# Packed attention scores, a later compressed branch, and moved angle, norm and down-product work in a hybrid attention and expert kernel

## The reference

```
h = RMSNorm(x);  proj = h @ w_in
A: 8 query heads, 2 kv heads, window 128, learned sinks, rotary      -> o_a
B: 8 query heads, 2 kv heads, rotary, three gated branches           -> o_b
     compressed: 31 blocks of 32 keys -> MLP (gelu, hidden 256) -> one key, one value each
     selected:   top 16 blocks of 64 keys (with 512 tokens that is every block)
     window:     512 keys
x = x + concat(o_a, o_b) @ w_out
x = x + PEER(RMSNorm(x)):  q = h @ w_query;  per head top 16 of 128 x 128 product keys,
     gelu(h . expert_down[e]) * gate, summed over expert_up[e]
y = RMSNorm(x) * norm_f
```

## Time and profile before

| | |
|---|---|
| time, median of 3 runs | 1576.52 us (1574.54 to 1577.93) |
| time of the profiled execution | 1576.16 us |
| its span | 1574.3 us |
| TensorE busy | 1530.9 us, 97% |
| VectorE busy | 1228.3 us, 78% |
| ScalarE busy | 613.6 us, 39% |
| GpSimd busy | 493.5 us, 31% |
| DMA | 374.27 MB, mean 238 GB/s |

### The profile page before, as it was taken

How to read it: one execution, slowest core, us unless ns; L and a number is a source line. 1 busy time by engine, 2 the same in 40 slices (tenths; PEclk the granted TensorE clock), 3 DMA queues, 4 the chain that set the end, 5 groups by cost and what they waited for, 6 DMA issues and landing times.

```text
span 1574.3 us, 22581 instructions
## 1 busy us (share of the span) xinstructions
PE 1530.9 (97%) x8493; PEld 1352.7 (86%) x8493; DVE 1228.3 (78%) x2289; ACT 613.6 (39%) x1033; POOL 493.5 (31%) x323
## 2 busy tenths in 40 slices
PE   7998999999999989999999999999999999999997
PEld 5876887888889989999888887999999999999996
DVE  6637766347999999993766765889888889888986
ACT  6215554352221335663333333333333333333334
POOL 0000000215674830002111111555554555555520
PEclk9999999999999999999999999999999999999999
DMA  4510000423321547899998998999999999999971
GB/s 176 214 54 1 2 1 1 177 100 118 128 71 59 169 134 278 319 339 330 310 311 294 304 307 292 348 366 358 372 362 365 350 365 361 375 360 362 354 256 67
DMA packets 147164, 374.27 MB, mean 238 GB/s; under 512 B 11728, under 2 KB 76368, under 8 KB 144112
## 3 DMA queue, kind: packets, MB, share of 16 engines
q1 hardware_dynamic: 99488, 197.66, 36.3%
q0 software_dynamic: 37200, 138.56, 24.0%
q10 hardware_dynamic: 10368, 36.60, 6.2%
HBM read 334.11 MB, written 38.67 MB: 237 GB/s over the span
## 4 chain that ended last, share of the span: by engine, by line
PE 70%; DVE 25%; DMA 3%; issue 1%; ACT 1%; SPq 0%; ACTq 0%; DVEq 0%
PE bank L1651 30%; PE bank L1344 30%; PE bank L1429 3%; PE bank L1510 2%; DMA a_e<-act_dram 2%; DVE oh L1245 2%; DVE oh L1248 2%; DVE gp L1250 2%; DVE gp L1253 2%; DVE cand L1183 1%; DVE d_lo L1234 1%; PE bank L1494 1%; DVE key L1138 1%; DVE work L1158 1%; DVE ti L1157 1%
## 5 line engine op out<-in xcount | busy, mean ns | idle before, releaser
L1344 PE MATMUL bank<-h_hi,d_hi 128*128 128x384 f32 x1024 | 348.9, 341 | 2.8 <-DVE d_lo L1234 1.7
L1344 PE MATMUL bank<-h_lo,d_hi 128*128 128x384 f32 x1024 | 346.5, 338 | 0.0
L1344 PE MATMUL bank<-h_hi,d_lo 128*128 128x384 f32 x1024 | 346.2, 338 | 0.0
L1651 PE MATMUL bank<-u_hi,w_hi_e 128*128 128x512 f32 x768 | 301.3, 392 | 5.1 <-DVE u_lo L1229 5.1
L1651 PE MATMUL bank<-u_lo,w_hi_e 128*128 128x512 f32 x768 | 300.9, 392 | 0.0
L1651 PE MATMUL bank<-u_hi,w_lo_e 128*128 128x512 f32 x768 | 299.7, 390 | 0.0
L506 POOL DMA_INDIRECT p_in<-rows,p_row x128 | 160.0, 1250 | 412.5 <-DVE p_dot L1272 190.4
L506 POOL DMA_INDIRECT p_in<-up,p_row x128 | 170.8, 1334 | 199.0 <-DVE p_dot L1272 96.6
L1344 PEld LDWEIGHTS bank<-h_hi,d_hi 128*128 128x128 f32 x1024 | 192.7, 188 | 6.7 <-DVE d_lo L1234 2.7
L1344 PEld LDWEIGHTS bank<-h_lo,d_hi 128*128 128x128 f32 x1024 | 192.8, 188 | 3.2
L1344 PEld LDWEIGHTS bank<-h_hi,d_lo 128*128 128x128 f32 x1024 | 192.6, 188 | 0.0
(11 more groups left out here) (243 smaller groups left out, 2372.5 us busy)
## 6 DMA issues: line engine op xcount, KB each, us to landing
d_raw<-down SPq DMA_DIRECT2D x128, 512.0 KB
u_raw<-up SPq DMA_DIRECT2D x128, 512.0 KB
gates_dram<-ev ACTq DMA_DIRECT2D x12, 2048.0 KB, 6.7
g_e<-gates_dram SPq DMA_DIRECT2D x32, 768.0 KB
w_raw<-wts SPq DMA_DIRECT2D x9, 2048.0 KB, 7.9
act_dram<-f_act ACTq DMA_DIRECT2D x58, 192.0 KB
a_e<-act_dram SPq DMA_DIRECT2D x58, 192.0 KB
xt<-x_in SPq DMA_DIRECT2D x4, 512.0 KB, 8.8
```

Source lines behind the costliest of these rows:

```text
L1344: m = nc.tensor.matmul(out, a, b, start=(n == 0 and j == 0), stop=(n == last and j == 2))
L1651: m = nc.tensor.matmul(bank[2 * b + half][:], w[e % 3][:, tok], u[:, half * COLS:(half + 1) * COLS], start=(e == 0 and j == 0), stop=(e == ...
```

## The change

1. *Packed scores.* `qp[g]` holds the high part of q in the 64 partitions of group g and its low part in the other 64; `k_hi[g]` holds the high part of k in both halves, `k_lo` the low part. One fp32r product over 128 rows gives high by high and low by high, a second over 64 rows gives high by low. The zeroing on GpSimd, `q_g1` and the split of tile 4 ahead of attention go.
2. *Later compressed branch.* Its keys and values are made at unit 6, its scores at units 26 and 31, its softmax on VectorE in steps 25 to 44, its products with the values at steps `C_AT` (46, 52, 58, 64) + 2. Blocks of `mixed` are transposed at `M_AT` (70 to 85). Tile 4 is split in eight pieces in steps 50 to 65 (`W4_AT`). The hidden weights of the values are loaded later, into another buffer.
3. *Angles* are computed behind the low parts of the first tile; their two DMAs move to SyncE's queue behind the first tile's.
4. *Slots.* E_SLOTS goes from 32 to 33, and with it E_DVE, NE and what hangs on them.
5. *Last norm.* Both sums first, then the gains; ScalarE scales the second half. TensorE's last products are reordered.
6. Some semaphores are merged.

```
-E_SLOTS = 32
+E_SLOTS = 33
-K_OF = {SWA: 0, SEL: 2, WIN: 3}
+K_OF = {SWA: 0, SEL: 1, WIN: 2}
+V_OF = {SWA: 0, SEL: 2, WIN: 3}
+K_CMP = 3
-M_STEPS = (9, 12)
+C_AT = [46 + 6 * qb for qb in range(TB)]
+C_LATE = 2
+M_AT = {70 + 6 * b + 3 * half: (b, half) for b in range(TB - 1) for half in range(2)}
+W4_AT = {50 + 2 * k: k for k in range(KC)}
...
-    q_g1 = place("q_g1", [P, 2, HPG, T], F32, base + 16384)
+    qp = [place("qp0", [P, 2, HPG, T], F32R, base + 3 * 16384), place("qp1", [P, 2, HPG, T], F32R, base + 16384)]
+    k_lo = place("k_lo", [P, 3, T], F32R, at[0])
+    k_hi = [sb(f"k_hi{g}", [P, 3, T], F32R) for g in range(GROUPS)]
...
             load_w0(3)
+            sp.dma_start(posi[:], pos).then_inc(S("freq_loaded"), 16)
+            sp.dma_start(cst[:, 384:432], consts[:, 384:432]).then_inc(S("freq_loaded"), 16)
...
+                if u == 14:
+                    act.wait_ge(S("evT"), 12)
+                    for g in range(GROUPS):
+                        for to in range(2):
+                            nc.scalar.activation(k_hi[g][DH * to:DH * to + DH], kT[DH * g:DH * g + DH, 0:3], ACT.Copy)\
+                              .then_inc(S("k_hi"), 1)
...
+                if s in W4_AT:
+                    k = W4_AT[s]
+                    if k == 0:
+                        act.wait_ge(S("w_loaded0"), 48)
+                        act.wait_ge(S("hid_done"), 2)
+                    nc.scalar.activation(w_hi[0][:, k], w_raw[0][:, k], ACT.Copy).then_inc(S("w_piece_hi"), 1)
...
+            def q_low(n):
+                for g in range(GROUPS):
+                    rows = slice(DH * g, DH * g + DH)
+                    other = slice(DH * (1 - g), DH * (1 - g) + DH)
+                    dve.wait_ge(S("q_hi"), 2 * n + g + 1)
+                    V.tensor_tensor(qp[g][other, n], qT[rows, n], f32(qp[g][rows, n]), ALU.subtract).then_inc(S("q_lo"), 1)
...
-                nc.tensor.matmul(bank[s % 3][:, 0:n], q_of[g][:, 0 if br == SWA else 1, j, qb * P:(qb + 1) * P],
-                                 kT[:, K_OF[br], k0:k0 + n], start=True, stop=False)
+                nc.tensor.matmul(bank[s % 3][:, 0:n], qp[g][:, which, j, tok], k_hi[g][:, K_OF[br], k0:k0 + n],
+                                 start=True, stop=False)
+                nc.tensor.matmul(bank[s % 3][:, 0:n], qp[g][own, which, j, tok], k_lo[own, K_OF[br], k0:k0 + n],
+                                 start=False, stop=False)
...
+                if s == 6:
+                    compress_out()
+                if s in (26, 31):
+                    compress_scores(s // 30)
...
                     V.tensor_tensor(o, o, bank[2 * b + half][:], ALU.add).then_inc(S("acc_done"), 1)
-                    dve.wait_ge(S("acc_done"), 2 * b + half + 1)
-                    V.tensor_tensor(xn[b % 2][:, parts[half]], o, nf[:, parts[half]], ALU.mult).then_inc(S("xn_done"), 1)
+                dve.wait_ge(S("acc_done"), 2 * b + 2)
+                for half in (1, 0):
+                    V.tensor_tensor(xn[b % 2][:, parts[half]], xt[:, b, parts[half]], nf[:, parts[half]], ALU.mult)\
+                     .then_inc(S("xn_done"), 1)
...
+                act.wait_ge(S("rstd_done"), 2 * TB + 2 + b)
+                act.wait_ge(S("xn_done"), 2 * b + 2)
+                nc.scalar.activation(xt[:, b, COLS:], xn[b % 2][:, COLS:], ACT.Copy, scale=rstd[:, b:b + 1])\
+                  .then_inc(S("y_half"), 1)
...
+                if e == NK - 1:
+                    for f in range(NK - E_TOK, NK - 1):
+                        add_expert(f, 1, 0)
```

More of the change, by code:

```diff
@@ L634, in _ @@
                   .then_inc(S("hid_act"), 1)
-            act.wait_ge(S("cmp_ps"), 1)
-            for g in range(GROUPS):
-                rows = slice(DH * g, DH * g + DH)
-                nc.scalar.activation(kcT[rows, g, 0:NC], bank[4][rows, 0:NC], ACT.Copy).then_inc(S("kc_done"), 1)
             def m_high(b, half):
@@ L648, in _ @@
                 qb, in_qb = divmod(s, STEP_QB)
-                if 1 <= qb < TB and in_qb in M_STEPS:
-                    m_high(qb - 1, M_STEPS.index(in_qb))
+                if s - 1 in M_AT:
+                    m_high(*M_AT[s - 1])
+                if s in W4_AT:
[4 more added lines that the diff above has]
+                    nc.scalar.activation(w_hi[0][:, k], w_raw[0][:, k], ACT.Copy).then_inc(S("w_piece_hi"), 1)
+                if s == 8:
+                    act.wait_ge(S("cmp_ps"), 1)
+                    for g in range(GROUPS):
+                        rows = slice(DH * g, DH * g + DH)
+                        nc.scalar.activation(kcT[rows, g, 0:NC], bank[7][rows, 0:NC], ACT.Copy).then_inc(S("kc_done"), 1)
                 if s < len(UNITS):
@@ L1323, in _ @@
                 dve.wait_ge(S("xn_done"), 2 * b + 2)
-                for half in range(2):
-                    V.tensor_scalar(xt[:, b, parts[half]], xn[b % 2][:, parts[half]], rstd[:, c], None, ALU.mult)\
-                     .then_inc(S("y_done"), 1)
+                V.tensor_scalar(xt[:, b, parts[0]], xn[b % 2][:, parts[0]], rstd[:, c], None, ALU.mult)\
+                 .then_inc(S("y_done"), 1)
         @block.tensor
@@ new lines, in compress_scores @@
+            def compress_scores(pair):
+                if pair == 0:
+                    pe.wait_ge(S("kc_done"), GROUPS)
+                    pe.wait_ge(S("vbd_done"), 8)
+                else:
+                    pe.wait_ge(S("c_masked"), 2)
+                for q in range(2 * pair, 2 * pair + 2):
+                    for j in range(HPG):
+                        c0 = (q % 2 * HPG + j) * GROUPS * CP
+                        m = nc.tensor.matmul(bank[7][:, c0:c0 + GROUPS * CP], qT[:, 1, j, q * P:(q + 1) * P],
+                                             kcT[:].rearrange("p g c -> p (g c)"), start=True, stop=True)
+                m.then_inc(S("c_s"), 1)
@@ L1550, in _ @@
                 if b == 0:
-                    pe.wait_ge(S("w_lo_done"), i + 1)
+                    if half == 0:
+                        pe.wait_ge(S("w_piece_lo"), 4 + KC)
+                    else:
+                        pe.wait_ge(S("w_lo_done"), 5)
                 if n >= 2:
```

285 lines of the change are left out of this document (149 added, 136 removed).

## The result

The changed kernel takes 1605.43 us (median of 4 runs, 1604.16 to 1612.14) against 1575.83 for the kernel before: a ratio of 1.0198, interval 1.0185 to 1.0211. It is 30 us slower where the prediction had 29 us faster. The profiled execution took 1612.14 us, its span is 1610.3, so its parts add up to 6 us more than the medians do.

What follows compares the result with a forecast made beforehand. TensorE was taken to bound wide attention units and the last phase, VectorE the key search and gates. Angles 1.0, attention 21.8, down products 5.3 and tail 1.3 make 29.4 us off 1576.16: 1546.8, forecast 1547, range 1541 to 1559.

Steps and rivals of the forecast that it cites:

- The second pass has 64 weight rows; I price it as a full one: Attention scores: the 64-row second product was priced like a 128-row fp32r pass, 0.230 us at 512 columns.
- the clock of 1.00: Attention: every stretch was priced with TensorE at its full granted clock; no term or rival allowed for a fall.
- The pair: Two fp32r products per score: 0.46, 0.35, 0.25 and 0.20 us at 512, 384, 256 and 128 columns.
- H2: Rival theory of the follow-up runs, attention scores: narrow fp32r product, or the type change from f32, costs 0.2 us extra.
- Narrow fp32r passes are dear: Rival for attention scores, chance 0.12: 128-wide steps become 0.96 less hidden waits, the others lose 2 us each; total 1557.5.
- 24.4 us of work saved: Attention: TensorE work saved by packed scores over 16, 16, 40 and 24 units at 512, 384, 256 and 128 columns.
- VectorE takes the middle: Rival, chance 0.2: VectorE bounds middle attention, total 1554.5; the forecast's sign was VectorE busier than TensorE in units 24 to 47.
- The later branch: Attention: moving the compressed branch out leaves 19 to 19.5 us for the 128-wide units; its work returns in later stretches.
- 33 down products: Ahead of the slot transposes: one more block fills TensorE's idle time, saving 4.2 us plus 1.1 from warm transposes, together 5.3.
- Angles: Start of the kernel: angle steps moved behind the first tile's low parts bring the first block's copies 1.0 us earlier (0.3 to 1.3).
- Tail: Last norm: output blocks every 4.3 us, six products pulled into the wait for the last low part; gain 1.3 us.
- DMA bounds the last phase: Rival, chance 0.03, slower side: expert gathers set the last phase; 5% more per expert cancels the gain, 6% gives 1581.

Runs made afterwards that it cites:

- g4: Changed kernel, 64-row second score products kept, first score product read as f32 at 128 and 256 keys: 1580.44 us, 1.0028 of the kernel before.
- h1: Changed kernel, full rows in the second score product, first read as f32 at 128 and 256 keys, six tail products ahead of the last wait: 1558.66 us.
- e1: Changed kernel with the second score product over all 128 rows instead of 64: 1560.88 us, 0.9908 of the kernel before.
- f3: Changed kernel, full rows at 128 and 256 keys; at 384 and 512 the second product keeps 64 rows, cut in two by columns: 1564.99 us, one run.
- f1: Changed kernel with full rows in the second score product and the first read as f32 at 128 keys: 1554.72 us, 0.9871 of the kernel before.
- g2: g1 with the eight low parts of tile 4 moved from VectorE to GpSimd: 1555.34 us, 0.9875 of the kernel before.
- e3: Changed kernel with plain f32 scores, one product over 128 rows, all other changes kept: 1567.25 us, 0.9946 of the kernel before.
- g3: Kernel before with only E_SLOTS raised from 32 to 33: 1569.95 us, 0.9963 of the kernel before.
- f2: Changed kernel with full rows in the second score product and six tail products ahead of the last expert's waits: 1560.93 us, 0.9907 of the kernel before.
- g1: Changed kernel with full rows, first score product read as f32 at 128 keys, six tail products ahead of the last wait: 1555.79 us, ratio 0.9867.
- h2: g1 with the f32 reading in units 0 to 47 (query blocks 0 and 1): 1556.26 us, 0.9875 of the kernel before.
- e4: Kernel before with its f32 score product over only the 64 rows of its group: 1622.57 us, 1.0297 of the kernel before.
- e2: Changed kernel without the second score product: 1556.71 us, 0.9879 of the kernel before.

## Why the prediction was wrong

The step that failed is "The second pass has 64 weight rows; I price it as a full one", and with it the clock of 1.00 that the sum of every stretch took for granted. The first was worth 20.6 us of the stage, the second the larger part, 36.0 us by subtraction.

*The pair.* Forecast 0.46, 0.35 and 0.20 at 512, 384 and 128 columns; measured 0.83, 0.72 and 0.49. At the full clock the rows are worth 20.6 us of the stage (g4 less h1). The Trainium skill (TensorE: Matmul & The Clock Gate, Step-by-step: what each phase is for) says that a weight load is pulled ahead of products in flight when the row groups don't conflict or when it goes to the background weight buffer. The traces show the pull and its loss, but not the first condition: a 128-row load goes ahead although the product in flight uses the same 128 rows (e1, 241.18), and so does a 64-row load behind a 64-row product (f3: two loads in 0.29 us from 248.76), while a 64-row load behind a 128-row product waits. Why that one waits no run shows. The Trainium skill (TensorE: Matmul & The Clock Gate, Single matmul latency) puts a product by itself at its columns plus about 175 ns; here, at a change of rows, it is 0.19 and 0.22 us over the columns. The length of a load, which the prediction weighed, is not it: with full rows two start 0.12 us apart (241.06 and 241.18).

*The clock.* The stage was 184.0 us. f1, full rows at a full clock, needs 127.4, the rows 20.6; the other 36.0 went with the granted clock, which was at half for some 106 us. That is an account by subtraction, with f1's 24 added passes left in, and g4 is part of it. What g4 shows directly is the least of it: same rows, full clock, more to stream, and a stage 28.9 us shorter. The prediction looked at TensorE's idle time and took the clock from the earlier trace rows. No rival of mine had a clock in it.

*The rest of the pair.* With full rows a pair is 0.55 and 0.33, not 0.46 and 0.25: the first product takes about 0.1 us over its columns, for a reason that no run looks for (it stands behind f32 products, so H2's "change of type" is still open for this part). With that, f1's stretches are 19.8, 31.9, 37.9 and 38.7 us against my 19 to 19.5, 29.5, 34.9 and 37.0. "Narrow fp32r passes are dear" is true only to that extent, 0.06 to 0.09 us a pair. (The prediction's 24.4 us of work saved adds up to 24.3 by its own figures.) Of "VectorE takes the middle" the sign that the prediction named did not show: in units 24 to 47 of f1 VectorE is busy for 25.85 us and TensorE for 27.72. In the third stretch it is not tile 4's split (g2). TensorE is idle for 4.2 and 2.6 us in the second and third stretch of f1, more than I gave the order of operations.

*The later branch.* e3 bears out the forecast: 19.24 us for the narrow units (19 to 19.5), and behind them 31.7 and 42.3 us of TensorE's work, where the prediction's sums for it without the savings of packing (25.6 + 5.8 and 33.4 + 7.5) make 31.4 and 40.9.

*33 down products.* Right: forecast 5.3, g3 5.9, idle 2.30 us (forecast 2.2), and in the changed kernel the last phase is one block shorter at the old spacing of 8.36 us. Whether the transposes are quick varies: 1.22 us in g3, 1.37 in the changed kernel, 2.19 in e1's chain of waits.

*Angles.* "So 1.0 us comes through" holds only where the weight piece is early. The mean square came at 5.26 in place of 6.96, but then (ScalarE's timeline):

```profile
9.25 1.06 ACT L552 ACTIVATE w_hi<-w_raw 128x1024 fp32r<-128x1024 f32 x1 [3.60 <-DMA w_raw<-wts]
10.21 1.12 ACT L567 ACTIVATE h_hi<-bank,prm 128x128 fp32r<-128x128 f32 x4
```

The copies start at 10.21 against 10.30. In the other runs with this start the cast began between 7.82 and 9.18, and the first score came 0.2 to 1.5 us earlier than before. The step had no range for the landing of a DMA.

*Tail.* Blocks every 4.2 us (forecast 4.3), and 0.1 us gained (30.76 to 30.64) in place of 1.3. "With six products pulled into the wait for the last low part" misread the code: they stand behind that wait. f2 puts them ahead and its tail is the 1.4 shorter.

*DMA bounds the last phase.* The only slower rival, and false: its share is 0.95, the blocks keep their 8.36 us.

What stays open: why the clock falls while TensorE is recorded as busy, and whether more passes or the f32 reading held it; why the same attention code keeps the clock in one execution and loses it in the next (f1 and g1), and why h1 spreads over 10 us at clocks of 0.994 to 0.998. The best versions, f1, g1, g2 and h2, lie at 1555 to 1556 with overlapping intervals, some 20 us under the kernel before and 50 under the changed one.

## What to carry to other kernels

Before cutting a product to the rows that it needs, look at its neighbours: between 128-row products a 64-row one costs two changes, and zeros (the kernel before against e4) or harmless terms (e1) in the unused rows cost less than the changes. Price TensorE by its steps from start to start, and ask of a change that thins its work what clock it will be granted; a stage in which TensorE is recorded as busy throughout can be at half speed. Where a forecast rests on what stands ahead of a wait, read the order of the lines.

## What the hardware showed

- One 64-row product between 128-row ones, at full clock, costs 0.23 us a unit at 128 columns and 0.28 to 0.29 at 256 to 512 (at 512 columns 0.40 and 0.43 against 0.32 and 0.23 with full rows), for both changes together; over 96 units it is 0.21 each, net of what waits hid. Two 64-row products in a row pay once (f3).
- The granted clock fell to 0.50 for over 100 us with TensorE recorded as busy all the time (98.00 of 98.00), and came back just ahead of the 384-wide units. Reading one product as f32, a pass more, in 64 of 96 units kept it at 1.00 and made the kernel 25.0 us faster; leaving a product out (e2) kept it low for longer than in e1.
- With plain f32 scores over 128 rows the clock was 1.00 in the narrow units of the kernel before and of e3, but for a short fall in g3's execution (0.66 from 155 to 160 us, behind 5 us in which TensorE was busy for 2.21); over 64 rows (e4) it fell to 0.50 from the first units on.
